# A gated-DeltaNet decoder layer: one piece of the gate projection at another place in the delta tile

## The chip, the cores and the metric

The kernel runs on one core of a Trainium2 chip (trn2). The metric is the device time of one execution in microseconds (us), the median of several runs.

A core has TensorE (PE in the profile; its weight loads are shown as PEld), VectorE (DVE), ScalarE (ACT), GpSimdE (POOL) and SyncE (SP, which here only issues DMAs). Each has its own list of instructions and runs it in the order written. Between engines the order is kept by semaphores alone.

## The reference

One layer of a hybrid decoder, for a prompt of 1024 tokens and 8 sample tokens, D_MODEL 1024, all in fp32:

```
proj = x @ w_in            # attention q/k/v, delta q/k/v, z, beta, a, two gates of 1024
A: dilated window attention, 3 groups of 4 heads x 64
B: gated DeltaNet, 4 heads, d_k = d_v = 128, chunked for the prompt:
   lower = tril_strict((k*beta) k^T * decay) + I
   sol   = lower^-1 [v*beta | k*beta*exp(gcum)]
   u = u0 - wk S;   o = q_dec S + attn u;   S = S*g_last + k_dec^T u
   o = o * rsqrt(mean(o^2)+eps) * w_norm * silu(z)
merged = sigmoid(gate1) * (A @ w_att_out) + sigmoid(gate2) * (B @ w_dn_out)
h = LN(alpha*x + merged @ w_o);   y = LN(alpha*h + ConvFFN(h))
```

It returns y of both groups and the new caches and states. Two parts matter here: branch B for the prompt, which is a chain from chunk to chunk with a matrix inverse in each, and `sigmoid(gate)`, whose 16 column blocks of 128 are plain projections that nothing in branch B needs.

## The kernel before

Every large product is in three matmuls: the fp32 operand is split into a high and a low part (`xh`, `xl`; `wh`, `wl`), both read as fp32r, and `xh*wh + xh*wl + xl*wh` is accumulated. The 1032 token columns are worked on in thirds of 344. A unit is one block of 128 output columns of a projection: three thirds of 24 matmuls each (8 blocks of the 1024 inputs, three matmuls for each), one PSUM bank for each third (`U[:, j]`).

The order of the work is written out by hand, for each engine separately, and it must agree between them. The stages are, in order, attention beside the q/k/v projections, the sample attention, the delta tiles 0 to 7 (first round at 549 us of the span; what is called tile 8 is only the end of tile 7's work beside a last unit, from 758 us), the sample part of branch B, the branch projections and the merge, the output projection and the first LayerNorm, and the ConvFFN.

**A delta tile** works on 128 tokens of all four heads. On TensorE (L1186 to L1264) tile i does this:

1. It turns the output of tile i-2 (`turned`, L1151: four transposes of `of`). They wait for `on_ready`, which VectorE gives after the scaling by the root (`out_scaled`, L2280).
2. It makes the two products of keys with keys and keys with queries (L1206, L1207).
3. It inverts the 128 x 128 unit lower triangle in six rounds (`for lv in range(LEVELS)`). Each round has a first small product into B56, a copy by ScalarE (`Y` or `Yw`), a second small product into B7, and an addition or copy by VectorE from which the next round starts. Rounds one to five work on 32 x 32 blocks, and round six on 64 x 64 blocks: its first product (L1230) waits for VectorE's copy into `Xw` (L2320), which waits for the first part of round five's second product (L1256; L1259 is the rest of it).
4. In rounds two, four and five it also does the state's products of the tile before (`state_read`, `updates`, `outputs`), and in round six it turns the attention output (L1242).

Between these stands one unit of the gate projection, cut into 18 **pieces** of four matmuls 128x128x344 (`quarter`, L1075 on TensorE): six pieces for each third. `Beside.run(n)` issues the next n pieces, `Beside.rest()` all that are left. Where they stand is the table `FILLS`, with one row for tiles with one unit (tiles 1 to 7) and one for tile 0, which has two. Its last two entries give the pieces after the first product of each round and the pieces after the second product of each round:

```
FILLS = {1: (0, 0, 4, 0, (1, 0, 1, 0, 0, 1), (1, 1, 1, 1, 0, 0)),
         2: (0, 0, 8, 0, (2, 0, 2, 0, 0, 2), (2, 2, 2, 2, 0, 0))}
```

So in tiles 1 to 7 pieces 1 to 4 stand before the first round, 5 to 10 in and between rounds one to five, piece 11 in round six, and pieces 12 to 18 at the end of the tile, before the transposes L1151 of the next one.

**ScalarE** walks through the same table (L1727 to L1788). A piece does nothing there, but for the last of each third, pieces 6, 12 and 18: there it waits until TensorE has finished the third, and writes `tanh(0.5*U)` to `gth` (L1629):

```
def quarter(u, par, j, c):
    if c == 5:
        act.wait_ge(slice_done, u * 3 + (j + 1))
        nc.scalar.activation(gth[:, par, third(j)], U[:, j, 0:TW], ACT.Tanh, scale=0.5)...
```

In round six ScalarE's list is: copy `Yw` (L1751), the pieces of this round, four scalings into `vp` (L1709). Behind the rounds stand the square of the output (L1715), the copy of the attention output (L1784), two squares of the next tile's keys and queries (L1670, L1671), and then the pieces of the end.

**VectorE** takes the sum of L1715's squares (L2274), the low part of the attention output (L2368), the sum of L1670's squares (L2216) and a few small ones, and then scales the output (L2280) as soon as GpSimdE has given the root (L859, which waits for L2275 behind L2274). L2280 is what the transposes L1151 of the next tile wait for. VectorE and GpSimdE do not use `FILLS`.

**SyncE** issues, in each tile, the loads for the next one; the load of `dv` (L665) waits for the scalings L1709, and behind it stand the store of the finished gate unit (L655, waits for the third Tanh) and the next weight load.

Of the kernel before, what the change touches and what calls it, by code (L numbers as in the profile page):

```python
# [91 lines left out]
def build(nc, I, O):  # L92
    ctx = ExitStack()
    with ctx:
# [254 lines left out]
        def after(eng, s, n):  # L349

            if not (isinstance(n, int) and n <= 0):
                eng.wait_ge(s, n)
# [101 lines left out]
                yield i, u, n  # L454
                u += n

        FILLS = {1: (0, 0, 4, 0, (1, 0, 1, 0, 0, 1), (1, 1, 1, 1, 0, 0)), 2: (0, 0, 8, 0, (2, 0, 2, 0, 0, 2), (2, 2, 2, 2, 0, 0))}

        def mix_slices():

# [501 lines left out]
        def _(pe):  # L962
# [223 lines left out]
            for i, u, units in tiles():  # L1186
                beside = Beside(u, u % 2, units, quarter, start_unit)
                f_turn, f_keys, f_mask, f_x, f_level, f_scan = FILLS[units]
                after(pe, xt_ready, i * (LEVELS + 1))
# [337 lines left out]
        def _(act):  # L1527
# [193 lines left out]
            def start_unless_last(last):  # L1721
                def start(u, par):
                    if u != last:
                        start_unit(u, par)
                return start

            for i, u, units in tiles():  # L1727
                last = u + units - 1
                beside = Beside(u, u % 2, units, quarter, start_unless_last(last if i < TILES else None))
                f_turn, f_keys, f_mask, f_x, f_level, f_scan = FILLS[units]  # L1730
                if i == TILES:
# [1161 lines left out]
```

## Time and profile before

| | |
|---|---|
| median of 3 runs | 1701.45 us (1701.43 to 1703.02) |
| the profiled execution: own time | 1699.52 us |
| its span, first to last instruction | 1697.7 us |
| mean granted TensorE clock | 0.995 |
| TensorE busy | 1668.3 us, 98% |
| VectorE, ScalarE, GpSimdE busy | 57%, 35%, 31% |
| one tile, L1151 of tile 2 to L1151 of tile 3 | 600.80 to 627.00 us |

Times in rows are us from the start of the span. A matmul's duration in a row is longer than the distance to the next matmul, because they overlap: the 128x344 ones are shown with 0.32 us and start about 0.16 us apart, so the cost of one in a stream is the distance between starts. "idle before <-releaser" in square brackets gives how long the engine stood idle before a row, and whose instruction ended that.

### The profile page before, as it was taken

Reading aid. Unit: us, or ns where it says so; the run is one execution under the profiler, and the core shown is the slowest. Engines: PE = TensorE matmul, PEld = TensorE weight load, DVE = VectorE, ACT = ScalarE, POOL = GpSimd, SP = SyncE. Lnnn points to the kernel's source line nnn. Section 1 sums busy time; section 2 is a strip of 40 time slices with the busy share of each in tenths; the row PEclk is TensorE's granted clock in tenths of the full one; section 3 lists DMA queues with packets and bytes.
Section 4 is the critical chain, followed back from the end, with each engine's and each line's share of the span. In section 5 each row is a group of like instructions: output and inputs, shape, how many; then the busy total and the mean of one; then the engine's idle time right before and its main releaser. Section 6 shows DMA issues by size and latency. Waiting matters only on the chain.

```text
span 1697.7 us, 35098 instructions
## 1 busy us (share of the span) xinstructions
PE 1668.3 (98%) x13967; PEld 1619.4 (95%) x13967; DVE 974.5 (57%) x1622; ACT 587.2 (35%) x1196; POOL 526.0 (31%) x287
## 2 busy tenths in 40 slices
PE   8999999999999999999999999999999999999996
PEld 7999999999999888889999999999999999999996
DVE  2002336778446577762764689877777777111157
ACT  3123334444432445452431462322222223301123
POOL 1221111111111022112432333655555554614320
PEclk9999999999999999999999999999999999999998
DMA  4111115455653343424771034444444416431202
GB/s 189 50 37 44 32 47 182 111 128 128 179 165 128 117 133 111 147 84 158 260 254 50 26 138 149 161 154 154 154 163 173 165 74 247 177 117 49 77 9 100
DMA packets 134576, 213.22 MB, mean 126 GB/s; under 512 B 60032, under 2 KB 100160, under 8 KB 132672
## 3 DMA queue, kind: packets, MB, share of 16 engines
q1 hardware_dynamic: 133472, 209.89, 37.3%
q10 hardware_dynamic: 1008, 1.98, 0.4%
q8 instruction: 69, 1.13, 0.3%
q14 instruction: 27, 0.22, 0.0%
HBM read 159.29 MB, written 79.95 MB: 141 GB/s over the span
## 4 chain that ended last, share of the span: by engine, by line
PE 94%; DVE 2%; DMA 2%; ACT 1%; issue 1%; SPq 0%; POOL 0%; ACTq 0%; DVEq 0%
PE U L970 35%; PE B L1451 16%; PE U L1075 10%; PE U L1451 6%; PE U L1372 5%; PE U L1519 3%; PE B L970 3%; PE B L1061 2%; PE B L1036 1%; PE B L1053 1%; PE B L1221 1%; PE B L1253 1%; DMA stage<-in_wu 1%; PE B L1044 1%; PE B L1163 1%
## 5 line engine op out<-in xcount | busy, mean ns | idle before, releaser
L850 POOL TENSOR_TENSOR wl<-stage,wh 128x1024 fp32r<-128x1024 f32 x81 | 195.1, 2409 | 743.7 <-ACT wh L1536 735.9
L970 PE MATMUL U<-xh,wh 128*128 128x344 f32 x960 | 314.1, 327 | 0.2 <-ACT qkv L1540 0.2
L970 PE MATMUL U<-xl,wh 128*128 128x344 f32 x960 | 307.6, 320 | 0.0
L970 PE MATMUL U<-xh,wl 128*128 128x344 f32 x960 | 307.6, 320 | 0.0
L970 PEld LDWEIGHTS U<-xh,wh 128*128 128x128 f32 x960 | 181.3, 189 | 0.6 <-ACT qkv L1540 0.5
L970 PEld LDWEIGHTS U<-xh,wl 128*128 128x128 f32 x960 | 181.3, 189 | 0.0
L970 PEld LDWEIGHTS U<-xl,wh 128*128 128x128 f32 x960 | 181.1, 189 | 0.0
L1536 ACT ACTIVATE wh<-stage 128x1024 fp32r<-128x1024 f32 x77 | 81.1, 1053 | 137.1 <-PE U L970 110.2
L1075 PE MATMUL U<-xl,wh 128*128 128x344 f32 x384 | 126.5, 329 | 0.0
L1075 PE MATMUL U<-xh,wh 128*128 128x344 f32 x384 | 125.7, 327 | 0.0
L1075 PE MATMUL U<-xh,wl 128*128 128x344 f32 x384 | 125.5, 327 | 0.0
L932 POOL TENSOR_TENSOR wl<-wsum,wh 128x512 fp32r<-128x512 f32 x57 | 90.1, 1594 | 51.8 <-ACT wh L1908 51.8
L2711 DVE SCALAR_TENSOR_TENSOR acc<-acc,U 128x344 f32 (+1 forms) x48 | 24.4, 513 | 139.4 <-PE U L970 138.2
L2532 DVE SCALAR_TENSOR_TENSOR cc<-ab,cst,cc 128x1024 f32<-128x1024 f32 (+2 forms) x52 | 92.7, 1784 | 5.6 <-DVE cc L2530 0.2
L970 PE MATMUL U<-hh,wh 128*128 128x344 f32 x280 | 90.1, 322 | 1.2 <-POOL hl L896 0.9
L1451 PE MATMUL B<-hh,qh 128*128 128x258 f32 x320 | 90.7, 284 | 0.4 <-DVE ab L2621 0.4
L1451 PE MATMUL B<-xh,wh 128*128 128x258 f32 x320 | 90.5, 283 | 0.0
L1451 PE MATMUL B<-hh,ql 128*128 128x258 f32 x320 | 90.4, 282 | 0.0
L1451 PE MATMUL B<-hl,qh 128*128 128x258 f32 x320 | 90.4, 282 | 0.0
L1451 PE MATMUL B<-xh,wl 128*128 128x258 f32 x320 | 90.2, 282 | 0.0
L1451 PE MATMUL B<-xl,wh 128*128 128x258 f32 x320 | 90.0, 281 | 0.0
L970 PE MATMUL U<-hh,wl 128*128 128x344 f32 x280 | 89.4, 319 | 0.0
(454 smaller groups left out, 4486.5 us busy)
## 6 DMA issues: line engine op xcount, KB each, us to landing
stage<-in_wu SPq DMA_DIRECT2D x126, 512.0 KB, 3.8
out_shift<-in_cache SPq DMA_DIRECT2D x16, 1022.0 KB
hid_scr<-cc SPq DMA_DIRECT2D x22, 516.0 KB, 2.9
gate_scr<-gth SPq DMA_DIRECT2D x16, 516.0 KB, 3.1
gates<-gate_scr SPq DMA_DIRECT2D x8, 1032.0 KB, 6.0
dn_scr<-thb SPq DMA_DIRECT2D x12, 512.0 KB, 2.8
tok_scr<-pre SPq DMA_DIRECT2D x48, 128.0 KB, 3.8
qkv<-in_cache SPq DMA_DIRECT2D x10, 512.0 KB, 5.9
```

Of the source, the lines that this page charges most:

```text
L850: nc.gpsimd.tensor_tensor(wl[:, par, :], stage[:, par, :], wh[:, par, :].bitcast(F32), ALU.subtract).then_inc(w_lo, 1)
L932: nc.gpsimd.tensor_tensor(l, SOURCE[p][0], fp(h), ALU.subtract).then_inc(q_low.sem, 1)
L970: ins = nc.tensor.matmul(dst, a[:, par, w], b[:, xk, third(j)], start=first and n == 0 and m == 0, stop=last and n == len(ks) - 1 and m == 2)
L1036: ins = nc.tensor.matmul(B34[:, hp, j * 256 + part * P:j * 256 + (part + 1) * P], q_st[rows, j, :], k_st[rows, (par + part) % 2, j, :], st ...
L1061: ins = nc.tensor.matmul(B7[:, 256 + 64 * h:256 + 64 * h + 64], pts[:, 2 * slot + part, :], vtok[:, (par + part) % 2, 64 * h:64 * h + 64], ...
L1075: ins = nc.tensor.matmul(U[:, j, 0:TW], a[:, par, k * P:(k + 1) * P], x[:, k, third(j)], start=m == 0, stop=m == 3 * KT - 1)
L1372: ins = nc.tensor.matmul(U[:, s % 3, 0:TW], w[:, k, :], x[:, k, third(j)], start=first and k == ks[0] and m == 0, stop=last and k == ks[-1 ...
L1451: ins = nc.tensor.matmul(bank[:, q, :], a[:, c], x[:, k, t], start=k == 0 and m == 0, stop=k == KH - 1 and m == 2)
L1519: ins = nc.tensor.matmul(U[:, s % 3, 0:TW], a[:, c], b[:, k, third(j)], start=k == 0 and m == 0, stop=k == ks[-1] and m == 2)
L1536: nc.scalar.activation(wh[:, par, :], stage[:, par, :], ACT.Copy).then_inc(w_hi, 1)
L2532: st.link(nc.vector.scalar_tensor_tensor(cc[:, a:a + w], ab[:, a + k:a + k + w], w3[k], cc[:, a:a + w], ALU.mult, ALU.add))
L2711: nc.vector.scalar_tensor_tensor(a, a, scale, U[:, j, 0:TW], ALU.mult, ALU.add).then_inc(used, 1)
```

## The change

```
-        FILLS = {1: (0, 0, 4, 0, (1, 0, 1, 0, 0, 1), (1, 1, 1, 1, 0, 0)), 2: ...}
+        FILLS = {1: (0, 0, 4, 0, (1, 0, 1, 0, 0, 1), (1, 1, 1, 1, 1, 0)), 2: ...}
```

The row of `FILLS` for tile 0 and everything else stay as they are. In tiles 1 to 7 one piece more is issued after the second product of round five, and one fewer at the end. As the pieces are numbered in the order of issue, piece 11 now stands between rounds five and six, piece 12 in round six, and pieces 13 to 18 at the end. Piece 12 is the last of the second third, so ScalarE's second Tanh moves too: from behind L1671 at the end of the tile to between L1751 and L1709 in round six. The number of instructions is the same on every engine.

## Rows read from the trace of the kernel before

**Rows 1.** The page: busy engines, and the chain that ended last.

```profile
PE 1668.3 (98%) x13967; PEld 1619.4 (95%) x13967; DVE 974.5 (57%) x1622; ACT 587.2 (35%) x1196; POOL 526.0 (31%) x287
...
PE 94%; DVE 2%; DMA 2%; ACT 1%; issue 1%; SPq 0%; POOL 0%; ACTq 0%; DVEq 0%
```

**Rows 2.** Waits, TensorE, 540 to 790 us: us in total, times, longest us.

```profile
PE B L1230 <- DVE Xw L2320: 1.5, 7, 0.2
```

**Rows 3.** Timeline, TensorE, end of tile 1: start us, us, engine, line, operation, out<-in.

```profile
593.36 0.35 PE L1259 MATMUL B<-XTq,Y 32*32 32x32 f32 x11
...
593.93 0.68 PE L1230 MATMUL B<-Xw,Loff 64*64 64x64 f32 x8 [0.22 <-DVE Xw L2320]
...
595.11 0.31 PE L1075 MATMUL U<-xh,wl 128*128 128x344 f32 x1
...
597.97 0.32 PE L1075 MATMUL U<-xh,wh 128*128 128x344 f32 x1
...
600.17 0.32 PE L1075 MATMUL U<-xl,wh 128*128 128x344 f32 x1
...
600.80 0.60 PE L1151 MATMUL B<-cst,of 128*128 128x128 f32 x4
```

**Rows 4.** Timeline, TensorE, tile 1, one piece and one small group.

```profile
585.96 0.43 PE L1075 MATMUL U<-xh,wl 128*128 128x344 f32 x1
...
586.79 0.45 PE L1253 MATMUL B<-XTq,Y 32*32 32x32 f32 x32
...
588.07 0.45 PE L1221 MATMUL B<-X,Lb 32*32 32x32 f32 x32
...
588.46 1.16 PE L1173 MATMUL B<-us,XT 128*128 128x128 f32 x8
```

**Rows 5.** Timeline, ScalarE, end of tile 1.

```profile
594.64 0.38 ACT L1751 ACTIVATE Yw<-B 64x256 f32<-64x256 f32 x1 [0.18 <-PE B L1230]
...
595.04 1.28 ACT L1709 ACTIVATE vp<-dv,rn 128x128 f32<-128x128 f32 x4
...
596.23 0.62 ACT L1715 ACTIVATE sqq<-of 128x512 f32<-128x512 f32 x1
...
598.19 0.45 ACT L1629 ACTIVATE gth<-U 128x344 f32<-128x344 f32 x1
```

**Rows 6.** Timeline, ScalarE, tile 2: a gate Tanh and its follower.

```profile
609.27 0.44 ACT L1629 ACTIVATE gth<-U 128x344 f32<-128x344 f32 x1
...
609.61 0.27 ACT L1749 ACTIVATE Y<-B 128x128 f32<-128x128 f32 x1
```

**Rows 7.** Timeline, GpSimdE and VectorE, end of tile 1.

```profile
597.84 1.01 POOL L859 TENSOR_TENSOR rn<-rn,mhalf 128x4 f32<-128x4 f32 x1 [0.94 <-DVE rn L2275]
...
596.88 0.69 DVE L2274 TENSOR_REDUCE rn<-sqq 128x4 f32<-128x512 f32 x1
...
599.34 0.69 DVE L2280 TENSOR_TENSOR of<-of,rn 128x512 f32<-128x512 f32 x1
```

**Rows 8.** Timeline, SyncE's queue, end of tile 1.

```profile
596.35 0.37 SPq L665 DMA_DIRECT2D dv<-tok_scr  x1
...
601.48 0.34 SPq L655 DMA_DIRECT2D gate_scr<-gth  x1
```

**Rows 9.** Timeline, end of tile 6, the last of six alike.

```profile
730.45 0.69 DVE L2280 TENSOR_TENSOR of<-of,rn 128x512 f32<-128x512 f32 x1
...
731.89 0.60 PE L1151 MATMUL B<-cst,of 128*128 128x128 f32 x4
```

**Rows 10.** Timeline, end of tile 7 and start of tile 8.

```profile
756.23 0.69 DVE L2280 TENSOR_TENSOR of<-of,rn 128x512 f32<-128x512 f32 x1 [0.78 <-POOL rn L859]
...
758.78 0.75 DVE L2285 SCALAR_TENSOR_TENSOR of<-B,onh,zin 128x512 f32<-128x512 f32 x1 [1.87 <-PE B L1151]
...
758.15 0.60 PE L1151 MATMUL B<-cst,of 128*128 128x128 f32 x4
...
759.68 1.13 PE L1163 MATMUL B<-S,dqk 128*128 128x128 f32 x8 [0.93 <-DVE of L2285]
```

More of the change, by code:

```diff
@@ L455, in tiles @@
                 u += n
-        FILLS = {1: (0, 0, 4, 0, (1, 0, 1, 0, 0, 1), (1, 1, 1, 1, 0, 0)), 2: (0, 0, 8, 0, (2, 0, 2, 0, 0, 2), (2, 2, 2, 2, 0, 0))}
+        FILLS = {1: (0, 0, 4, 0, (1, 0, 1, 0, 0, 1), (1, 1, 1, 1, 1, 0)), 2: (0, 0, 8, 0, (2, 0, 2, 0, 0, 2), (2, 2, 2, 2, 0, 0))}
         def mix_slices():
```

## The prediction

> **What bounds the kernel.** I read the page first: TensorE is busy 98% of the span and carries 94% of the chain that ended last [rows 1]. So each us that TensorE gains or loses inside the delta tiles moves the end by the same, as long as what follows them waits on their own results and not on a clock of its own. The other engines matter only where TensorE waits for them. Next I read the waits of TensorE over the tiles: the place that the change fills is there, idle before round six's first product L1230, seven times, 1.5 us in all, 0.2 us each, ended by VectorE's copy L2320 [rows 2]. Last I read the timelines of all engines at the end of a tile, because the piece is taken from there: what it covered there has to be found. TensorE does not wait at L1151 in any tile [rows 3, 9, 10]; the question is by how much.
>
> **Part 1: the piece added before round six.** Round five's second product is shown to end at 593.36 + 0.35 = 593.71. After such a small group the next one starts 0.06 before the shown end (588.07 + 0.45 = 588.52, next at 588.46) [rows 4], so TensorE is free for the piece at 593.65. A piece between two small groups takes 586.79 - 585.96 = 0.83 from its start to that of the next group [rows 4]. L1230 then starts at 594.48, where it started at 593.93 [rows 3]: 0.55 later. VectorE's copy, for which L1230 now stands idle 0.22 us, is long done by then, so this wait is gone. What it is replaced by is 0.83 of work; the whole distance that the piece fills was only 0.28. Bounds: if it starts at the last shown end, 0.61 later; if its edges cost nothing (0.63, below), 0.35 later.
>
> The TensorEngine Tiling (Array Packing) page of the Trainium skill, section Key Properties, says that changing the tiling mode, as from 32x32 to 128x128 blocks, drains TensorE. That speaks against the change, since the piece adds such a change where there was one (32 to 64). The rows agree in size: 0.83 for a piece between small groups against 0.63 in a stream. Without that loss L1230 would be 0.35 late and TensorE alone would win 0.28 in each tile; with it, it wins 0.08.
>
> **Part 2: the piece removed at the end.** In the stream of pieces 14 matmuls take 600.17 - 597.97 = 2.20 [rows 3], 0.157 each, so four take 0.63. If nothing else waited, L1151 would start 0.63 - 0.55 = 0.08 earlier in each tile, 0.6 us over seven tiles. No DMA is in a piece, and the third's bank is read as before.
>
> **Part 3: ScalarE's second Tanh.** Pieces are counted in the order of issue, so the one that now stands in round six is piece 12, which ends a third. ScalarE meets its Tanh in round six, behind L1751 and ahead of L1709, and must wait for TensorE to finish piece 12. Before, L1709 starts 595.04, right behind L1751 [rows 5]. Piece 12 stands where piece 11 stood, right behind L1230; its last matmul is shown to end at 595.11 + 0.31 = 595.42, 1.49 after L1230's start [rows 3]. With L1230 at 594.48 that is 595.97. ScalarE starts 0.03 after TensorE's end (L1230 ends 594.61, L1751 starts 594.64) [rows 3, 5], so the Tanh starts at 596.00. The next instruction starts 609.61 - 609.27 = 0.34 behind a Tanh's start [rows 6]: L1709 at 596.34, **1.30 late**: 0.55 from TensorE, 0.75 from the Tanh and the wait for its piece.
>
> Behind L1709 stand on ScalarE, without a gap, L1715 (596.23), the copy L1784, and L1670; the Tanh that now has left came after all of these, at 598.19, where nothing behind it was in a hurry [rows 5]. Who waits for them: VectorE's L2274 starts 596.88, 0.03 after L1715 ends at 596.85, and from there to L2280 it works through its list almost without a gap, 599.34 - 596.88 = 2.46 us [rows 5, 7]. GpSimdE's root, 597.84 to 598.85, is inside this stretch and is not what L2280 waits for [rows 7]; it moves along. So L2280 starts at 600.64 and ends at 601.33.
>
> **Part 4: what is late next.** L1151 starts at 600.80, and L2280 ends at 600.03 [rows 3, 7]. A product that truly waits for VectorE starts 0.15 after the end (758.78 + 0.75 = 759.53, L1163 at 759.68) [rows 10], so the spare time is 0.62 before the change and 0.54 with one piece fewer at the end. So L1151 starts at 601.33 + 0.15 = 601.48, not at 600.72: TensorE stands idle for about 0.76 us, and the tile is longer by 0.68. The distances at the end of tile 6 are the same: L2280 at 730.45, L1151 at 731.89, 1.44 apart, where tile 1 has 1.46 [rows 9]; tiles 1 to 6 are alike. 6 x 0.68 = 4.1 us.
>
> Tile 7 has no next tile's keys to square and sum, so its L2280 comes after the root, at 756.23. It moves to 757.53, ends 758.22, and L1151 starts at 758.37 where it was at 758.15 [rows 10]: 0.2 us.
>
> Everything behind L1151 in the next tile (L1206, L1207, the masks, the rounds) waits on TensorE's own products, so it moves with it and neither wins back nor adds. SyncE: the load of `dv` goes out at 596.35 behind L1709, and the next thing on its queue is the store at 601.48, behind the third Tanh [rows 8]. 1.3 us later is inside that gap of 5.1, and `dv` is used a tile later. If that cover were gone, a weight load would start later by what is over.
>
> Sum: 4.1 + 0.2 = **+4.3 us**. On the profiled execution that is 1697.7 to 1702.0 of span, 1699.5 to 1703.8 of own time. The runs' median is 1.9 above this execution's time, and the difference is carried over: 1701.45 + 4.3 = 1705.7. Its own range comes from the bounds. Low: L1230 late by 0.35, so L1709 by 1.10, and L1151 starts 0.06 behind L2280's end in place of 0.15 (0.06 is the edge in [rows 4]); then 0.39 for each of six tiles and nothing for tile 7, 2.3 us. High: L1230 late by 0.61, so L1709 by 1.36; 0.74 for six tiles and 0.28 for tile 7, 4.7 us. I take the middle because each term has a row of the same form.
>
> The PSUM — Partial Sum Buffer page of the Trainium skill, section Engine vs sequencer instructions, calls ScalarE's queue "strict FIFO". The rows show the same: L1709 with its inputs ready starts behind L1751 and not before. If ScalarE could run L1709 ahead of a Tanh that waits, only the 0.55 of L1230 would arrive at L2280, which would end at 600.58, at the very edge of the spare time, and the result would be the -0.6 us of part 2.
>
> **Rivals.**
>
> A, **not slower**: the cover at the end holds. L2280 does not reach L1151, because the stretch from L1751 to L2280 closes up by 0.7 us or more (the starts of its instructions are partly apart by the way of a signal, not by work). Then only TensorE's own sum counts: -0.6 us, and at the most 7 x (0.63 - 0.35) = -2.0, so 1700.8 (down to 1699.5). It decides at a lateness of L2280 of 0.54, up to which L1151 isn't touched, and up to 0.62 the tile isn't longer. For it: the idle time before L1230 does go [rows 2], and it is the only wait for work between the rounds five and six. Against it: 1.30 is twice 0.62, the 0.75 of it that the Tanh makes is already more, and L1709 to L1715 is without a gap (1.28 shown, 1.19 from start to start) [rows 5].
>
> B, **much slower**: the lateness does not stay at what TensorE loses, because late ScalarE and VectorE meet further waits in the next tile, the masks before round one above all. Then up to the whole 1.30 comes back in each of seven tiles: +9.1 us, 1710.6. It decides where an instruction of the next tile's start needs L2280's followers, and not L1151, as the last. For it: VectorE has its own sums of the next tile's keys ahead of L2280. Against: in tile 8 VectorE stands idle 1.87 us for L1151 itself [rows 10], and after L1151 it needs TensorE's L1207 before the masks.
>
> **Chances.** Forecast 0.76; A 0.14; B 0.06; something that I don't see 0.04. A measurement of this kernel can tell about 0.2% from no change, 3.4 us. The forecast is above that by only 0.9 us, so I give a fifth of its chance to "within 0.2%". Slower: 0.76 x 0.8 + 0.06 + 0.01 = 0.68. Within: 0.76 x 0.2 and nearly all of A, 0.28. Faster: the 0.04 that is left, of A's low end and of what I don't see. The predicted time is the forecast's, 1705.7; the range 1702.4 to 1707.6 takes in its bounds (2.3 to 4.7 us, with up to 1.3 for the runs' scatter, which is 1.6 before) and leaves out most of A and B.
>
> **What would show it.** In the changed kernel's timeline of a tile's end: the piece right behind L1259 and no idle time before L1230; L1230 0.5 to 0.6 us later against L1259; on ScalarE a Tanh between L1751 and L1709, and L1709 1.15 us after L1751 in place of 0.40; L2280 ended 6.85 after L1230's start (594.48 to 601.33) in place of 6.10; and a new wait on TensorE, L1151 for L2280, six times some 0.7 us and once 0.2. If that wait isn't there, parts 3 and 4 are wrong and A holds. If it is and tiles are longer by more than about 0.8, B has a part in it.

## The result, and the profile after

| | before | changed |
|---|---|---|
| median of 20 runs | 1700.9 us | 1705.7 us |
| range of the runs | 1698.5 to 1704.1 | 1703.7 to 1707.6 |
| ratio, 95% interval | | 1.0030 (1.0024 to 1.0037) |
| span of the profiled execution | 1697.7 us | 1704.4 us |
| L1151 of tile 2 to L1151 of tile 8 | 157.35 us | 161.46 us |

The changed kernel is slower by 4.8 us. The spans of the two profiled executions differ by more, 6.7 us: 0.3 of it is there before the tiles begin, it has grown to 5.1 at L1151 of tile 8, and the rest comes after the tiles, in stages that the change does not touch.

The page of the changed kernel, to be held against [rows 1]: its instructions are the same in number, TensorE's busy time has not moved in any way that matters, but its share of the chain is 89% in place of 94%, and VectorE's 5% in place of 2%.

```profile
PE 1670.0 (98%) x13967; PEld 1619.5 (95%) x13967; DVE 975.2 (57%) x1622; ACT 586.3 (34%) x1196; POOL 526.3 (31%) x287
...
PE 89%; DVE 5%; DMA 2%; ACT 2%; issue 1%; SPq 0%; POOL 0%; ACTq 0%; DVEq 0%
```

TensorE's waits over the tiles (us in total, times, longest), against [rows 2]: the wait of L1230 for VectorE's copy has gone, and a wait of L1151 for the scaling L2280 has come, seven times. The second row was there before, too (0.93 in [rows 10]).

```profile
PE B L1151 <- DVE of L2280: 4.6, 7, 0.7
...
PE B L1163 <- DVE of L2285: 0.9, 1, 0.9
```

TensorE at the end of tile 1 (start us, us, line, operation), against [rows 3]. All starts are 0.34 later than before from earlier stages, so distances are to be compared: L1230 starts 1.10 after the last L1259's row in place of 0.57, and L1151 7.03 after L1230 in place of 6.87, though there is one piece fewer between.

```profile
593.70 0.35 PE L1259 MATMUL B<-XTq,Y 32*32 32x32 f32 x11
...
593.98 0.42 PE L1075 MATMUL U<-xh,wl 128*128 128x344 f32 x1
...
594.80 0.67 PE L1230 MATMUL B<-Xw,Loff 64*64 64x64 f32 x8
...
595.99 0.32 PE L1075 MATMUL U<-xl,wh 128*128 128x344 f32 x1
...
596.15 0.38 PE L1242 MATMUL B<-cst,ao 128*128 128x128 f32 x2
...
596.46 0.68 PE L1262 MATMUL B<-XT,Yw 64*64 64x64 f32 x8
...
600.78 0.32 PE L1075 MATMUL U<-xl,wh 128*128 128x344 f32 x1
...
601.83 0.63 PE L1151 MATMUL B<-cst,of 128*128 128x128 f32 x4 [0.72 <-DVE of L2280]
```

ScalarE in the same stretch, against [rows 5]: the Tanh L1629 stands between the copy L1751 and the scalings L1709, and idles 0.46 for piece 12 first. L1709 starts 1.18 after L1751 in place of 0.40.

```profile
595.52 0.38 ACT L1751 ACTIVATE Yw<-B 64x256 f32<-64x256 f32 x1 [0.72 <-PE B L1230]
...
596.35 0.46 ACT L1629 ACTIVATE gth<-U 128x344 f32<-128x344 f32 x1 [0.46 <-PE U L1075]
...
596.70 1.27 ACT L1709 ACTIVATE vp<-dv,rn 128x128 f32<-128x128 f32 x4
...
597.87 0.62 ACT L1715 ACTIVATE sqq<-of 128x512 f32<-128x512 f32 x1
```

VectorE, against [rows 7]: L2280 starts 7.06 after the copy L2320, where it was 5.75 (599.34 - 593.59).

```profile
593.93 0.28 DVE L2320 COPY Xw<-B 32x128 f32<-32x128 f32 x1 [1.17 <-PE B L1256]
...
598.53 0.69 DVE L2274 TENSOR_REDUCE rn<-sqq 128x4 f32<-128x512 f32 x1 [0.94 <-ACT sqq L1715]
...
600.99 0.69 DVE L2280 TENSOR_TENSOR of<-of,rn 128x512 f32<-128x512 f32 x1
```

The end of tile 6, and of tile 7, against [rows 9, 10]: the wait before L1151 is the same in the last of six alike, and 0.27 in tile 7, where VectorE's list is shorter.

```profile
736.77 0.63 PE L1151 MATMUL B<-cst,of 128*128 128x128 f32 x4 [0.72 <-DVE of L2280]
...
762.45 0.69 DVE L2280 TENSOR_TENSOR of<-of,rn 128x512 f32<-128x512 f32 x1 [0.78 <-POOL rn L859]
...
763.29 0.63 PE L1151 MATMUL B<-cst,of 128*128 128x128 f32 x4 [0.27 <-DVE of L2280]
```

The start of the copy L2320, which is given by TensorE's round five, is the same point in each tile of each kernel, so distances from it can be set side by side. This table takes them, in us, from the timelines; the run of each row is described below. They agree within 0.02 us over tiles 1 to 6 of a kernel. The last column is the difference in the distance to L1151, the part of the tile that the edits touch:

| kernel, tiles 1 to 6 | L1709 | L2280 | L1151 | L1151 against before |
|---|---|---|---|---|
| before | 1.46 | 5.75 | 7.21 | |
| changed | 2.77 | 7.06 | 7.90 | +0.69 |
| piece alone, Tanh at the end | 2.00 | 6.29 | 7.13 | -0.08 |
| Tanh behind the scalings | 2.00 | 6.77 | 7.61 | +0.40 |
| before, L1709 0.40 late | 1.87 | 6.15 | 7.21 | 0 |
| before, L1709 0.81 late | 2.27 | 6.55 | 7.39 | +0.18 |
| before, L1709 1.18 late | 2.64 | 6.92 | 7.76 | +0.55 |
| changed, two copies more | 3.17 | 7.46 | 8.30 | +1.09 |
| changed, output scaling first | 2.77 | 6.60 | 7.43 | +0.22 |
| changed, scalings last | 4.60 | 6.02 | 7.01 | -0.20 |
| the same, Tanh at the end | 4.22 | 6.02 | 7.01 | -0.20 |

In each row L1151 is the later of two things: TensorE's own arrival (7.21 in the old order, 7.01 in the new) and L2280's start + 0.84.

The other part of a tile, from L1151 to the next copy, is 18.98 to 19.06 us before. In most kernels one or two tiles have 0.1 to 0.6 more there, mostly at one group of 32x32 matmuls. Such a group is in tile 3 of the changed kernel (0.77 us in place of 0.45), and in tile 3 of the kernel before with two needless copies, too (0.78), so it does not come from the change.

### The profile page after: what moved, and what is told of

It reads as the page before. It is cut to its first block, busy times and chain, and to the rows that moved or that the text cites. A ratio compares the mean times of both kernels' runs of the same rounds, so it can differ in the third digit from the quotient of the medians.

```text
span 1704.4 us, 35098 instructions
## 1 busy us (share of the span) xinstructions
PE 1670.0 (98%) x13967; PEld 1619.5 (95%) x13967; DVE 975.2 (57%) x1622; ACT 586.3 (34%) x1196; POOL 526.3 (31%) x287
## 3 DMA queue, kind: packets, MB, share of 16 engines
q8 instruction: 69, 1.13, 0.3%
## 4 chain that ended last, share of the span: by engine, by line
PE 89%; DVE 5%; DMA 2%; ACT 2%; issue 1%; SPq 0%; POOL 0%; ACTq 0%; DVEq 0%
PE U L970 34%; PE B L1451 15%; PE U L1075 9%; PE U L1451 6%; PE U L1372 5%; PE U L1519 3%; PE B L970 3%; PE B L1061 2%; PE B L1036 1%; DMA stage<-in_wu 1%; PE B L1053 1%; PE B L1221 1%; PE B L1253 1%; ACT vp L1709 1%; PE B L1044 1%
## 5 line engine op out<-in xcount | busy, mean ns | idle before, releaser
L970 PE MATMUL U<-hl,wh 128*128 128x344 f32 x280 | 89.3, 319 | 0.0
```

Source lines behind the costliest of these rows:

```text
L970: ins = nc.tensor.matmul(dst, a[:, par, w], b[:, xk, third(j)], start=first and n == 0 and m == 0, stop=last and n == len(ks) - 1 and m == 2)
```

## The experiments

### The piece alone

```
# TensorE as changed; ScalarE's walk keeps the old table for tiles 1 to 7
+                f_scan = f_scan[:4] + (f_scan[4] if units == 2 else 0, f_scan[5])
```

> TensorE's order is the changed one (piece 11 between rounds five and six), but ScalarE keeps its second Tanh at the end of the tile, as before. My theory (the Tanh ahead of the scalings L1709 makes most of the lateness): L1709 is late only by what round six is late, 0.53 us, which the spare time of 0.62 at the end holds. No wait at L1151, or under 0.05 us; each tile is 0.05 to 0.1 us shorter than before, 7 tiles -0.6 us, time within 0.1% of before. Rival (TensorE's own cost, the change of tiling mode and the filled gap, makes the tile longer wherever ScalarE's Tanh stands): +4 to +5 us, as the change.

Measured: ratio 0.9998 (0.9989 to 1.0007). VectorE's copy and scaling, and TensorE's transposes, in tile 1:

```profile
591.47 0.28 DVE L2321 COPY Xw<-B 32x128 f32<-32x128 f32 x1 [1.17 <-PE B L1256]
...
597.76 0.69 DVE L2281 TENSOR_TENSOR of<-of,rn 128x512 f32<-128x512 f32 x1
...
598.60 0.63 PE L1151 MATMUL B<-cst,of 128*128 128x128 f32 x4
```

L1709 is late by 0.54 only, L1151 stands 7.13 after the copy, no wait is listed before it, and the rival is out: with TensorE in exactly the changed order, the loss is gone. The forecast gain of 0.6 us is too small for the runs' times; the tiles of the profile have 0.08 each. But L1151 starts just 0.84 after L2280, the distance that a true wait has, so here it comes at the very moment when it may. That is 0.12 later than TensorE could (7.01, last rows of the table), and the weight loads stand idle there 1.2 us in all over six tiles, with no releaser named.

### ScalarE's lateness without the piece

```
# before; n = 4, and in a later run n = 2
+                        for m in range(n if i > 0 else 0):
+                            nc.scalar.activation(dum[:, m, :], ident, ACT.Copy)
                         value_sides(i)
```

`dum` is a buffer that nothing reads.

> The kernel before with no piece moved. In tiles 1 to 7 ScalarE does four needless copies of 128x128 (constants into a buffer that nothing reads) between L1751 and L1709. My theory: L1709 and all behind it are late by 4 x 0.30 = 1.2 us, L1151 waits for L2280, and the tile is 0.57 us longer (1.2 less the spare 0.62), tile 7 some 0.1: +3.5 us. Rival (the moved piece is needed for the loss): 0.

Measured: ratio 1.0006 (0.9997 to 1.0015), +0.18 in each of six tiles. The number that I expected was wrong, because the copies were: four start within 0.81 us, 0.20 each, not 0.30.

```profile
594.85 0.91 ACT L1782 ACTIVATE dum<-cst 128x128 bf16<-128x128 f32 x4
...
595.66 1.26 ACT L1710 ACTIVATE vp<-dv,rn 128x128 f32<-128x128 f32 x4
```

The rule held for what was really added: 0.81 less 0.62 is 0.19. The ScalarE: Activation LUTs page of the Trainium skill, section What ACT_TABLE_LOAD costs, gives an ACTIVATE with immediate scale and bias 186 ns + 0.833 ns for each column, about 93 ns more for each pointer operand, and an overlap of about 93 ns between neighbours. For 128 columns an estimate from that page is 186 + 107 - 93 = 200 ns, and the trace agrees: 0.81 / 4 = 0.20 us. The next run has scalings from a pointer in their place, as L1709 has them:

```
# before
+                        if i > 0:
+                            act.wait_ge(k_rooted, i + 1)
+                        for m in range(4 if i > 0 else 0):
+                            nc.scalar.activation(dum[:, m, :], ident, ACT.Identity, bias=0.0,
+                                                 scale=rn[:, 2, m:m + 1])
```

> The kernel before with no piece moved, and in tiles 1 to 7 four needless scalings of 128x128 ahead of L1709 (the form of L1709 itself, 0.30 us from start to start; the plain copies of the run before took 0.20 each, so that run made L1709 only 0.80 late). My theory: L1709 is 1.19 late, L1151 starts 1.19 - 0.62 = 0.57 later in each of six tiles, some 0.1 in tile 7: +3.5 us against before. Rival (a part of the change's loss needs the piece between the rounds): the tile grows by clearly less than 0.57.

Measured: ratio 1.0020 (1.0011 to 1.0030), +0.55 for each of six tiles and 0.10 in tile 7, 3.4 us. ScalarE's two rows, and TensorE's waits (in this kernel the transposes are line 1152):

```profile
595.18 1.28 ACT L1784 ACTIVATE dum<-cst,rn 128x128 bf16<-128x128 f32 x4
...
596.37 1.27 ACT L1710 ACTIVATE vp<-dv,rn 128x128 f32<-128x128 f32 x4
...
PE B L1152 <- DVE of L2285: 2.3, 6, 0.4
```

No piece is moved here, and the loss per tile is all but 0.14 of the change's, which is how much less L2280 is late (1.17 in place of 1.31).

> The kernel before with two needless copies of 128x128 ahead of L1709, 0.40 us. This is under the spare time of 0.62. Theory: no tile is longer by more than 0.05; 0 us. Rival (each us of ScalarE at this place counts): +0.4 in each of seven tiles, +2.8 us.

Measured with two copies: ratio 0.9998 (0.9988 to 1.0008). L2280 is 0.40 late and L1151 is where it was to 0.01 us. So below the spare time lateness costs nothing, and above it each us of lateness costs one.

### More of it on top of the change

```
# changed
+                        for m in range(2 if i > 0 else 0):
+                            nc.scalar.activation(dum[:, m, :], ident, ACT.Copy)
                         value_sides(i)
```

> The changed kernel with two needless copies of 128x128 ahead of L1709 in tiles 1 to 7, 0.40 us in all. My theory: the spare time is used up, so ScalarE's lateness goes one to one into the tile: 0.40 us in each of seven tiles, +2.8 us against the changed kernel, +7.6 against before. Rival (L1151's wait has another last releaser than the chain over ScalarE): less than half of that.

Measured: ratio to before 1.0043 (1.0027 to 1.0058), and the tile is 0.40 longer than the changed one. The wait before the transposes has grown from 4.6 to 7.4 us, 0.40 for each:

```profile
PE B L1152 <- DVE of L2283: 7.4, 7, 1.1
```

### Where the Tanh stands

```
# changed; ScalarE's walk without the piece between the rounds
                     if lv == 5:
                         value_sides(i)
+                        if i > 0:
+                            beside.run(1)
```

> As the change, but ScalarE's second Tanh stands behind the scalings L1709 and ahead of the square L1715. Piece 12 is long done there, so the Tanh costs only its 0.34 us and no wait for TensorE. My theory: L1715 is late by 0.53 + 0.34 = 0.87, that is 0.25 over the spare time: 0.25 us in each of six tiles, nothing in tile 7, +1.4 us. If only the wait for the piece mattered it would be -0.6; if the Tanh costs the same wherever it stands ahead of L1715, +4.8.

Measured: ratio 1.0009 (1.0000 to 1.0018); 0.40 for each of six tiles, -0.07 in tile 7. L2280 is 1.02 late and not the 0.87 that I expected, so the tile is 0.40 longer and not 0.25:

```profile
PE B L1151 <- DVE of L2283: 2.6, 6, 0.4
```

ScalarE's square was 1.01 late: 0.54 of round six, 0.35 of the Tanh, and some 0.12 between scalings, Tanh and square (a Tanh right behind the scalings starts 1.31 after them, where the square had started 1.19 after them). The Tanh costs its own time wherever it stands ahead of the square, and ahead of the scalings the wait for its piece comes on top.

### The other links of the chain

```
# changed; on VectorE
                 if i > 1:
                     out_scaled(i - 2)
+                if i > 0:
+                    key_norms(i)
                 masks(i)
...
-                if i + 1 < TILES:
-                    key_norms(i + 1)
```

> The changed kernel with VectorE's sums of the next tile's keys (L2216 to L2220) moved behind the scaling of the output L2280. ScalarE's late Tanh stays. My theory: VectorE's own list is the last link of the chain to L1151; with it out of the way L2280 waits for GpSimdE's root only and starts 0.44 earlier (600.55 in place of 600.99 in tile 1), so the wait at L1151 falls from 0.72 to about 0.3. But the masks come later: the gated output L2285 and the mask L2239 then start some 0.2 us late, which can show as a wait before round one. Tile 0.25 to 0.45 longer than before (the change: 0.70), +1.8 to +3.0 us against before. Rival (VectorE's sums are beside the path): as the change, +4.8.

Measured: ratio 1.0012 (1.0001 to 1.0023), the tile 0.22 to 0.27 longer than before. In tile 1 (this kernel's times are its own):

```profile
597.86 0.69 DVE L2280 TENSOR_TENSOR of<-of,rn 128x512 f32<-128x512 f32 x1 [0.78 <-POOL rn L859]
...
598.70 0.63 PE L1151 MATMUL B<-cst,of 128*128 128x128 f32 x4 [0.27 <-DVE of L2280]
...
600.48 0.74 DVE L2285 SCALAR_TENSOR_TENSOR of<-B,onh,zin 128x512 f32<-128x512 f32 x1
```

L2280 now waits for GpSimdE's root alone and starts 6.60 after the copy in place of 7.06. The gated output L2285 now starts 1.78 after L1151 in place of 0.66, which is later than I expected, but the mask L2239 starts 2.52 after L1151 in both kernels, and the wait of the weight loads before round one is the same 1.5 us in all as before: the moved sums cost nothing there. So VectorE's sums of the next keys were a link of the chain, and moving them wins back two thirds of the loss.

```
# changed; ScalarE's scalings behind the squares of the next keys
-                    if lv == 5:
-                        value_sides(i)
...
                 if i + 1 < TILES:
                     squares(i + 1)
+                value_sides(i)
                 beside.rest()
# GpSimdE, norm_root, and VectorE, key_norms
+                after(pool, vp_ready, t)
+                after(dve, k_rooted, t)
```

> The change with the scalings L1709 moved on ScalarE behind the squares of the next tile's keys (L1670, L1671), for which GpSimdE's root of the keys waits for them and VectorE's sum waits for that root. The early Tanh stays in round six. My theory: L1715 comes right behind the Tanh, about 0.1 us late against before in place of 1.3; L2280 is early enough; no wait at L1151; -0.6 us against before. Rival (a late end is due to the Tanh's own wait on TensorE or to VectorE): the wait at L1151 stays and it is +4 us or more.

Measured: ratio 0.9990 (0.9981 to 0.9999). No wait at L1151, and L1151 is 0.20 nearer to the copy than before, though the early Tanh is still there.

The last run of this group joins this edit with ScalarE's old table of the piece alone.

> As the run with the scalings last, but the second Tanh stands at the end of the tile as before: piece between the rounds, nothing ahead of the square L1715. Theory: no wait at L1151, L2280 another 0.2 to 0.4 earlier than there, and the tile 0.2 shorter than before, the same as there: 7 x 0.2 = 1.4 us faster than before. Rival (that run's small gain came from elsewhere): the tile as long as before.

Measured: ratio 0.9987 (0.9978 to 0.9996), 1698.6 us against 1701.2 beside it. Tile 1, from the copy to the transposes (in this kernel L1716 is the square L1715, L2337 the copy L2335, L2276 the sum L2274):

```profile
591.22 0.28 DVE L2322 COPY Xw<-B 32x128 f32<-32x128 f32 x1 [1.17 <-PE B L1257]
...
593.47 0.63 ACT L1716 ACTIVATE sqq<-of 128x512 f32<-128x512 f32 x1 [0.28 <-DVE of L2272]
...
594.47 0.42 DVE L2337 COPY XT<-B 64x256 f32<-64x256 f32 x1 [1.03 <-PE B L1263]
...
594.81 0.67 DVE L2276 TENSOR_REDUCE rn<-sqq 128x4 f32<-128x512 f32 x1
...
597.25 0.69 DVE L2282 TENSOR_TENSOR of<-of,rn 128x512 f32<-128x512 f32 x1
...
598.23 0.60 PE L1152 MATMUL B<-cst,of 128*128 128x128 f32 x4
```

L1151 is 7.01 after the copy. L2280 is no earlier than with the early Tanh, 6.02 in both, though the square starts 0.52 earlier (2.25 after the copy in place of 2.77). The sum of the squares is what holds it: it stands on VectorE behind the copy of round six's second product, which waits for TensorE, and starts 3.58 to 3.59 after the first copy in both kernels. So the 0.2 to 0.4 that I expected of L2280 is not there, and L1151 is where I expected it.

These two are faster than before and than the change. The edits' share of that is 0.20 in each of seven tiles, 1.4 us. In the two profiled executions the tiles as a whole are only 0.8 and 0.4 us shorter than before, because some of them have up to 0.6 more between L1151 and the next copy; why, no run shows. No run has the scalings last without the moved piece. The old order's 7.21 for TensorE's own arrival speaks against a gain there, but that is argued and not measured.

### The other wait that went

In the changed kernel L1242 starts 1.35 after L1230 in place of 1.42, and the transposes' group takes 0.31 in place of 0.34. In the old order the weight loads before it stood idle 0.2 us in each tile, with no releaser named:

```profile
PEld B L1242 <- issue: 1.2, 7, 0.2
```

VectorE's new state L2268 starts 0.93 after the copy L2320, in tile 1 at 594.52, and lasts 0.69; L1242 starts at 595.35, which is 0.14 after its end.

In tile 0, where there is no state of a tile before, the same group starts 0.15 behind its piece even before the change:

```profile
568.84 0.32 PE L1075 MATMUL U<-xh,wh 128*128 128x344 f32 x1
...
568.99 0.38 PE L1242 MATMUL B<-cst,ao 128*128 128x128 f32 x2
```

```
# before
                     if lv == 4 and i > 0:
+                        nc.vector.tensor_tensor(dum[:], ident, ident, ALU.add)
                         new_state(i - 1)
```

> The kernel before with one needless sum of 128x128 on VectorE (0.3 us) ahead of the state's update L2268. The traces show that with the piece between the rounds the short idle time of the weight loads before L1242 is gone, and that TensorE gains 0.2 us in a tile in place of 0.1. Theory: L1242 waited there for L2268 (both in B34), which the later round six covers. Then L2268 0.3 us late makes L1242 0.3 late and the tile 0.3 longer, +2.1 us. Rival (the idle time belongs to the kind of matmul ahead of it): L1242 and the tile stay within 0.05.

Measured: the tiles not disturbed otherwise are 0.30 longer, L1243 (the same transposes) starts 1.73 after the first product of round six in place of 1.42, and now the releaser is named:

```profile
PE B L1243 <- DVE S L2269: 6.0, 7, 2.4
```

So L1242 did wait for VectorE's new state. But the kernel was slower by 12 us (ratio 1.0073, 1.0058 to 1.0089) and not by 2.1. In the profiled execution, 11.3 slower, tiles 3 and 7 have 5.2 and 3.7 us more than the other five, because something else happened there. Here are the needless sum and GpSimdE's subtraction of the weights in tile 2, and then in tile 3:

```profile
618.65 0.29 DVE L2365 TENSOR_TENSOR dum<-cst 128x128 f32<-128x128 f32 x1
...
618.67 2.51 POOL L851 TENSOR_TENSOR wl<-stage,wh 128x1024 fp32r<-128x1024 f32 x1 [20.90 <-ACT wh L1537]
...
645.41 2.37 POOL L851 TENSOR_TENSOR wl<-stage,wh 128x1024 fp32r<-128x1024 f32 x1 [21.14 <-ACT wh L1537]
...
645.44 2.48 DVE L2365 TENSOR_TENSOR dum<-cst 128x128 f32<-128x128 f32 x1
```

In the five tiles like tile 2 the sum starts 0.01 to 0.02 us first, takes its 0.29, and GpSimdE's row is 2.51 to 2.52 long in place of 2.37. In tiles 3 and 7 GpSimdE starts 0.03 first and takes its 2.37, and the sum takes 2.48 and ends 0.14 behind GpSimdE's end. The SBUF — State Buffer page of the Trainium skill, section SBUF: two separate sides, calls the port pair that VectorE and GpSimdE share an exclusive lock, which a VectorE operation with two SBUF inputs takes for the whole instruction against a GpSimdE operation that reads SBUF; this trace agrees.

```
# as the run before, one operand in PSUM
+                        dve.wait_ge(od_done, i)
+                        nc.vector.tensor_tensor(dum[:], ident, B34[:, 0, 0:P], ALU.add)
```

> In the run with the late state update, VectorE's needless sum of two SBUF operands took 2.48 us in place of 0.29 in tiles where GpSimdE's subtraction L851 had started 0.03 us before it. Here the sum stands at the same place with one operand in PSUM. Theory (two SBUF operands of VectorE and GpSimdE's work exclude one another): the sum takes 0.3 us in every tile, the tile is 0.3 longer than before, +2.1 us, no tile with 2 us more. Rival (anything of VectorE that starts behind GpSimdE waits): 2.5 us again in some tiles and about +10 us.

Measured: ratio 1.0004 (0.9994 to 1.0013). In the seven tiles the sum takes 286 to 290 ns, also where GpSimdE starts 0.04 ahead of it:

```profile
647.93 2.38 POOL L851 TENSOR_TENSOR wl<-stage,wh 128x1024 fp32r<-128x1024 f32 x1 [21.18 <-ACT wh L1537]
...
647.97 0.29 DVE L2366 TENSOR_TENSOR dum<-cst,B 128x128 f32<-128x128 f32 x1
```

The tile is 0.20 longer than before, not 0.30. The sum again takes 0.29, but the next instruction, the new state, starts 0.20 after it in place of 0.31, so the state is only 0.20 late (1.13 after the copy in place of 0.93). The transposes are 0.20 late as well, where the run before had 0.31 and 0.31: their wait follows the state one to one.

## Why the prediction was right

**The time.** Forecast 1705.7, +4.3 us; measured 1705.7, +4.8. That the two times are the same is luck: the forecast started from 1701.45, 0.5 above the median of the 20 runs, and its step was 0.5 too small. The profile's own sum over tiles 1 to 7 is 0.69 + 0.71 + 0.97 + 0.73 + 0.72 + 0.72 + 0.26 = 4.8. About 0.3 of it is the long group of small matmuls in tile 3, which is not the change's; the other 4.5 is to be held against the 4.3. The upper end of the range is 0.1 above its own terms (1701.45 + 4.7 + 1.3 = 1707.45), which decides nothing.

**Part 1, the piece costs more than its gap.** L1230 0.55 later forecast, 0.53 measured (0.87 after the copy in place of 0.34). The piece starts 0.28 after the last L1259's row starts (0.29 forecast) and takes 0.82 to L1230 (0.83 forecast); the 0.22 wait is gone. What makes up the 0.2 that a piece costs more here than in a stream, no run separates.

**Part 2, TensorE's own gain.** Forecast 0.08 a tile, measured 0.20. This is the one term that was wrong in its mechanism: it took the stretch from L1230 to the end as rigid. The stretch held a second wait, L1242's for VectorE's new state, which the late round six covers. From L1230 to the second product L1262 it was 1.76 and is 1.66, which is 0.10 of the missing 0.12; the other 0.02 is L1230's 0.53 in place of 0.55. The wait is shown by the two runs with the late state, the 0.20 by the two runs with the scalings last. The error did not move the forecast time, because L1151 waits for VectorE either way; it moved rival A's, -1.4 and not -0.6, and the spare time, 0.42 and not 0.54.

**Part 3, ScalarE's Tanh.** L1709 late 1.30 forecast, 1.31 measured; L2280 late 1.30 and 1.31. The piece alone shows 0.54 of it as round six's, and the Tanh with its wait as the other 0.77.

**Part 4, what is late next.** L1151 0.68 late forecast, 0.69 measured, tile 7 0.22 and 0.22. The 0.15 from VectorE's end to the waiting matmul was right: in every kernel that waits, L1151 starts 0.69 + 0.15 = 0.84 after L2280's start. That SyncE and the next tile neither add nor win back is shown by the extra copies: 0.40 on ScalarE is 0.40 in the tile, and no other wait appears.

**Rivals.** A did not come: the chain from L1751 to L2280 did not close up (4.70 before, 5.47 now, longer by the Tanh and its wait), and there is a clean threshold at 0.62 of lateness in the old order (0.40 free, 0.81 costs 0.18, 1.18 costs 0.55). B did not come either: only what is above the threshold is lost, and it is lost once in a tile.

## What to carry to other kernels

Work that fills a wait is taken from somewhere, and there it covered a wait too: before a piece is moved, look up how early the thing it covered was ready (here 0.62 us), and how late the move makes it. Where several engines walk through one table, a moved item takes its followers on every engine along; here the item itself was right where it was put, and what cost was the Tanh that the count brought with it into the middle of another chain. Leave such followers where they were, or put work that nobody waits for soon (here four scalings) behind work that somebody does wait for: the same edit was then a gain of about 0.1% (ratio 0.9990, 0.9981 to 0.9999) in place of a loss of 0.3%.

## What the runs showed of the hardware

**A VectorE sum of two SBUF operands and GpSimdE's subtraction exclude one another** (2.48 us in place of 0.29; with one operand in PSUM 0.29 in all seven tiles). Whether GpSimdE starts 0.03 us before the sum or 0.01 after it decides if VectorE loses 2.2 us, and that can differ between repetitions of the same loop body.

**TensorE's granted clock fell to half after that short wait.** In tile 3 of the run with the late state TensorE stood idle for 2.4 us, from 646.4 to 648.8. Windows: us, busy and instructions of PE, PEld, DVE, ACT and POOL, PEclk, DMA share, GB/s. In the stretches behind it the granted clock is 0.50 and 0.51, which is 1.2 GHz, and from 655.5 on it is 1.00, 2.4 GHz.

```profile
646.00:648.70 2.70, 0.36 (x3) 0.07 (x1) 2.69 (x3) 1.25 (x4) 1.78 (x1) 0.98 0.05 16
...
648.70:652.00 3.30, 3.23 (x15) 2.81 (x16) 1.98 (x6) 2.10 (x5) 0.20 (x1) 0.50 0.23 67
...
652.00:655.50 3.50, 3.50 (x14) 3.50 (x14) 2.52 (x8) 0.41 (x1) 1.81 (x2) 0.51 0.00 0
...
655.50:660.00 4.50, 4.50 (x36) 4.48 (x35) 1.06 (x3) 1.09 (x2) 0.00 (x0) 1.00 0.32 109
```

Tile 3 was 5.2 us longer than the undisturbed ones, and only some 2.2 of that was the wait; the other 3 went in the stretch at 1.2 GHz, where the 128x344 matmuls start 0.29 us apart in place of 0.157. The same wait in tile 7 was followed by a granted clock of 0.50 from 762 to 764 us. No other wait in the tiles of any run, up to 1.1 us, had that follow it.
